# Attention with its branch and output products taken per two query tiles, as seven half products for eight

## The reference

```python
a = dsa_attention(q, k, v, qi, ki, wi, k_sel) * jax.nn.silu(z_a)
b = multiscale_pool(u_b, pool_w[layer], pool_scale[layer]) * jax.nn.silu(z_b)
g = jax.nn.sigmoid(gates.reshape(B, S, N_BRANCHES, D_MODEL) + merge_bias[layer])
y = g[:, :, 0] * (a @ w_branch_a[layer]) + g[:, :, 1] * (b @ w_branch_b[layer])
x = x + y @ w_out[layer]
```

## Time and profile before

| | |
|---|---|
| median of 3 runs | 3606.58 us (3606.16 to 3606.78) |
| span of the profiled execution, first to last instruction | 3598.9 us |
| what the runs have around that span | 7.7 us |
| TensorE busy | 3489.8 us, 97% of the span |
| VectorE, ScalarE, GpSimd busy | 1897.1, 1626.0, 416.8 us |
| start of `attention` to the end | 2709.4 to 3598.9, that is 889.5 us |

### The profile page before, as it was taken

How to read it: one execution, slowest core, us unless ns; L and a number is a source line. 1 busy time by engine, 2 the same in 40 slices (tenths; PEclk the granted TensorE clock), 3 DMA queues, 4 the chain that set the end, 5 groups by cost and what they waited for, 6 DMA issues and landing times. The chain is left out here.

```text
span 3598.9 us, 70546 instructions
## 1 busy us (share of the span) xinstructions
PE 3489.8 (97%) x28700; PEld 2709.4 (75%) x28700; DVE 1897.1 (53%) x4784; ACT 1626.0 (45%) x3703; POOL 416.8 (12%) x690
## 2 busy tenths in 40 slices
PE   6999999996999999999999999999999999999998
PEld 5888988885666666578778887777886677777765
DVE  5223332346777777534788788666683333333322
ACT  2222333324445444313677666777763334443320
POOL 0000000004554544310000000000000000000000
PEclk9999999998999999999999999999999999999999
DMA  9111111114222222241111114121215212111121
GB/s 310 60 48 54 54 54 54 54 76 139 72 92 91 82 77 77 91 132 48 50 54 62 53 52 168 57 66 61 69 47 194 79 48 78 42 50 67 50 82 41
DMA packets 142357, 282.08 MB, mean 78 GB/s; under 512 B 35056, under 2 KB 94464, under 8 KB 134528
## 3 DMA queue, kind: packets, MB, share of 16 engines
q1 hardware_dynamic: 133360, 267.75, 21.3%
q0 software_dynamic: 2304, 8.39, 0.6%
q10 hardware_dynamic: 6416, 2.08, 0.2%
HBM read 181.72 MB, written 96.47 MB: 77 GB/s over the span
## 5 line engine op out<-in xcount | busy, mean ns | idle before, releaser
L2598 ACT ACTIVATE at_pT<-at_bank 128x512 f32<-128x512 f32 (+3 forms) x320 | 154.4, 531 | 532.1 <-PE at_bank L2497 531.8
L1992 PEld LDWEIGHTS p_bank<-p_hT,w_in_rest 128*128 128x128 f32 x3072 | 345.4, 192 | 14.0 <-issue 12.4
L1992 PE MATMUL p_bank<-p_hT,w_in_rest 128*128 128x128 f32 x3072 | 349.9, 276 | 1.3 <-DVE p_st L2276 1.3
L325 PE MATMUL p_bank<-p_hT,w_in_rest 128*128 128x128 f32 x2720 | 349.1, 275 | 0.0
L325 PEld LDWEIGHTS p_bank<-p_hT,w_in_rest 128*128 128x128 f32 x2720 | 326.4, 192 | 0.0
L2113 ACT ACTIVATE p_r<-p_acc,p_mid 128x384 f32<-128x384 f32 (+13 forms) x224 | 292.9, 1308 | 58.7 <-DVE p_acc L2303 54.4
L1983 PE MATMUL p_bank<-arena,p_hT 128*128 128x512 f32 (+2 forms) x768 | 242.8, 468 | 1.3 <-ACT p_hT L2107 1.3
L2538 PE MATMUL at_bank<-arena,at_y 128*128 128x512 f32 x512 | 239.8, 599 | 4.1 <-DVE at_y L2648 2.5
L2173 ACT ACTIVATE p_r<-p_bank,ahead_rows 128x512 f32<-128x512 f32 (+3 forms) x304 | 168.1, 635 | 156.2 <-PE p_bank L2086 144.3
L325 PE MATMUL p_bank<-p_hT,arena 128*128 128x128 f32 x1632 | 229.0, 276 | 4.0 <-ACT p_hT L421 3.0
L2074 PE MATMUL p_bank<-p_hTg,arena 128*128 128x256 f32 x1024 | 226.7, 381 | 1.7 <-ACT arena L2135 1.7
(11 more groups left out here) (428 smaller groups left out, 6264.5 us busy)
## 6 DMA issues: line engine op xcount, KB each, us to landing
stage<-p_st SPq DMA_DIRECT2D x15, 1856.0 KB, 5.9
arena<-stage SPq DMA_DIRECT2D x15, 1856.0 KB, 7.6
at_rest<-stage SPq DMA_DIRECT2D x16, 1280.0 KB, 5.9
stage<-x_or_pr SPq DMA_DIRECT2D x128, 128.0 KB, 1.8
p_ada<-in_ada_w SPq DMA_DIRECT2D x8, 1024.0 KB, 9.6
p_xt<-in_x SPq DMA_DIRECT2D x16, 512.0 KB, 3.2
x_or_pr<-in_x SPq DMA_DIRECT2D x16, 512.0 KB, 3.2
x<-x_or_pr SPq DMA_DIRECT2D x16, 512.0 KB, 3.3
```

Of the source, the lines that this page charges most:

```text
L325: last = mm(out, w_in(k, at, at + P), hT[:, k, 1:P + 1], start=(k == 0), stop=(k == KD - 1))
L1992: last = mm(bank[:, m * P:(m + 1) * P], weights(k, c + m * P, c + (m + 1) * P), hTs[:, n % 2, k, :], start=(k == 0), stop=(k == KD - 1))
L2598: f(flat(pT[:, g, at // P:(at + wide) // P, :]), TURNED[j % 2][:, 0:wide], ACT.Copy).then_inc(S["pT_taken"], 1)
```

## The change

The dense products are no longer made per tile but per pair of tiles that follow each other in `ORDER` (e = 0, 1). For a product of a pair, the activation (256 tokens by the contraction) and the weight are each cut into 2 x 2 blocks, and Strassen's scheme in Winograd's form replaces the eight block products by seven. The seven half products of a kind are named by a digit: b1 to b7, a1 to a7, p1 to p7. A branch half product has 8 matmuls of 128 columns, an output one 4 matmuls of 512 columns. So a pair has 14 branch and 7 output products, where it had 8 branch halves of 16 matmuls and 4 output halves of 8.

- **Weights.** The sums of weight blocks are made once, in the gate phase: SP loads 16 pieces (4 of b, 4 of a, 8 of the output weight; four blocks of 256 columns each), POOL makes four sums of 128 x 256 for each, and SP stores them to a DRAM tensor `combined`. One piece is begun at every seventh chunk n, and stored four chunks later. The attention reads `combined` in 14 slots of 1 MB per pair (two branch products share a slot, an output product has one) through a ring of 5 slots, so 14 MB per pair and 112 slots in all.
- **Activations.** POOL makes four sums of 128 x 256 for b and for a (`T`), and four of 128 x 512 for y (`Sy`).
- **Results.** DVE takes each product out of PSUM and adds it into its block (`take`, 24 instructions per pair where there were 16); the gates, the sum of both branches and the sum with x go from DVE to POOL: `gated_b`, `gated_a`, `out_sum`.
- **Order.** The dense products of pair m run in the eight steps of the tiles of pair m+1, two or three in a step, by the tables `DENSE_EARLY` and `DENSE_LATE`; eight steps after the last tile serve the last pair alone. From the last pair of tiles on (`DENSE_LATE`), the uses rotate over three banks, two of them taken from the four score banks; until then all share one as before. The first product of a step stands ahead of the values product, except where d does.

```diff
+                def fetch_piece(e):
+                    kind, part = PIECES[e]
+                    if e == 0:
+                        sp.wait_ge(S["zb_done"], TILES)
+                    from_one(sp, S["piece_stored"], 16 * e)
+                    load = lambda dst, src: sp.dma_start(dst, src).then_inc(S["piece_loaded"], 16)
+                    k, at = part // 2, part % 2 * PIECE_W
+                    for i, (row_half, column_half) in PIECE_PLACES[kind]:
...
+                            load(pieces[:, i, :], A["w_out_2"][0][(4 * row_half + k) * P:(4 * row_half + k + 1) * P, c:c + PIECE_W])
+                        elif kind == "b":
+                            load(pieces[:, i, :], A["w_branch_b_2"][0][(2 * row_half + k) * P:(2 * row_half + k + 1) * P, c:c + PIECE_W])
+                        else:
+                            for g in range(A2_KV):
+                                r = 256 * g + HEAD * (2 * row_half + k)
+                                load(pieces[HEAD * g:HEAD * g + HEAD, i, :], A["w_branch_a_2"][0][r:r + HEAD, c:c + PIECE_W])
...
+                def store_piece(e):
...
+                    sp.wait_ge(S["piece_combined"], e + 1)
+                    sp.dma_start(combined[:, at:at + 7 * w].rearrange("p (i w) -> p i w", w=w)[:, :, part * PIECE_W:(part + 1) * PIECE_W], pieces[:, 0:7, :]).then_inc(S["piece_stored"], 16)
...
+                        if n >= 2 and n - 2 < 7 * len(PIECES):
+                            if (n - 2) % 7 == 0:
+                                fetch_piece((n - 2) // 7)
+                            if (n - 2) % 7 == 4:
+                                store_piece((n - 2) // 7)
...
+                def combine(e):
...
+                    if PIECES[e][0] == "o":
+                        tt(part(3), part(6), part(7), ALU.subtract)
+                        ch.link(tt(part(5), part(7), part(0), ALU.subtract))
+                        ch.link(tt(part(2), part(6), part(5), ALU.subtract))
+                        tt(part(4), part(2), part(1), ALU.subtract).then_inc(S["piece_combined"], 1)
...
+HALVES = (1, 2, 6, 7, 4, 5, 3)
...
+LATE_PAIR = PAIRS - 1
+DENSE_EARLY = (("b1", "b2", "b6"), ("b7", "b4", "b5"), ("b3", "a1", "a2"), ("a6", "a7", "a4"), ("a5", "a3", "p1"), ("p2", "p6"), ("p7", "p4"), ("p5", "p3"))
+DENSE_LATE = (("b1", "b6", "b7"), ("b2", "b5", "b4"), ("b3", "a1", "a6"), ("a7", "a2", "a5"), ("a4", "a3", "p1"), ("p2", "p6"), ("p7", "p5"), ("p4", "p3"))
+LATE_BANK = {"d": 0, "1": 0, "2": 0, "6": 1, "7": 2, "5": 1, "4": 2, "3": 1}
...
+                def fetch_x(m):
+                    from_one(sp, S["out_stored"], 32 * m)
+                    for e in range(2):
+                        load("x_loaded", o[:, e, :], x1[rows_of(ORDER[2 * m + e]), :])
+
+                def fetch_weights(k):
+                    if k >= RING_W:
+                        sp.wait_ge(S["spare_done"], USES.last_of_slot[k - RING_W])
+                    at = k % SLOTS_W * SLOT_W
+                    load(f"w_loaded{k % RING_W}", ring[:, k % RING_W, :], combined[:, at:at + SLOT_W])
...
+                for step in range(STEPS + BLOCKS_OF):
...
+                        fetch_za(n)
+                    if step % BLOCKS_OF == 2 and 2 <= step // BLOCKS_OF <= PAIRS:
+                        fetch_x(step // BLOCKS_OF - 1)
+                    if step % BLOCKS_OF == 5 and 1 <= step // BLOCKS_OF < PAIRS:
+                        fetch_rest(step // BLOCKS_OF)
+                    while fetched < SLOTS_W * PAIRS and step >= BLOCKS_OF and USES.last_of_slot[fetched - RING_W] <= max(place[name, step // BLOCKS_OF - 1] for name in dense_of(step)) + 1:
+                        fetch_weights(fetched)
+                        fetched += 1
...
+                def moving_sums(half):
+                    tt(T[:, 2, :], half(1, 1), half(1, 0), ALU.subtract)
+                    ch.link(tt(T[:, 0, :], half(1, 0), half(0, 0), ALU.subtract))
+                    ch.link(tt(T[:, 1, :], half(1, 1), T[:, 0, :], ALU.subtract))
+                    tt(T[:, 3, :], T[:, 1, :], half(0, 1), ALU.subtract).then_inc(S["T_ready"], 1)
+
+                def stationary_sums(m):
+                    pool.wait_ge(S["y_added"], 4 * m + 4)
+                    from_one(pool, S["spare_done"], place["p3", m - 1] + 1 if m > 0 else 0)
+                    y11, y12, y21, y22 = (y[:, e, k, :] for e in range(2) for k in range(2))
+                    ch.link(tt(Sy[:, 0, :], y21, y22, ALU.add))
+                    ch.link(tt(Sy[:, 1, :], Sy[:, 0, :], y11, ALU.subtract))
+                    tt(Sy[:, 2, :], y11, y21, ALU.subtract)
+                    tt(Sy[:, 3, :], y12, Sy[:, 1, :], ALU.subtract).then_inc(S["Sy_ready"], 1)
+
...
+                def gated_b(name, m):
+                    e, half = WHERE[name[1]]
+                    pool.wait_ge(S["spare_taken"], place[name, m] + 1)
+                    tt(yb[:, e, half, :], yb[:, e, half, :], gate("b", e, half), ALU.mult).then_inc(S["yb_ready"], 1)
+
+                def gated_a(name, m):
+                    e, half = WHERE[name[1]]
+                    pool.wait_ge(S["spare_taken"], place[name, m] + 1)
+                    pool.wait_ge(S["yb_ready"], 4 * m + 4)
+                    ch.link(tt(y[:, e, half, :], y[:, e, half, :], gate("a", e, half), ALU.mult))
+                    tt(y[:, e, half, :], y[:, e, half, :], yb[:, e, half, :], ALU.add).then_inc(S["y_added"], 1)
+
+                def out_sum(name, m):
+                    e, half = {"p2": (0, 0), "p4": (1, 0), "p5": (1, 1), "p3": (0, 1)}[name]
+                    part = yb[:, half, e, :]
+                    c = slice(512 * half, 512 * half + 512)
+                    pool.wait_ge(S["spare_taken"], place[name, m] + 1)
+                    pool.wait_ge(S["x_loaded"], 32 * (m + 1))
+                    tt(o[:, e, c], o[:, e, c], part, ALU.add).then_inc(S["o_added"], 1)
...
+                def spare_for(name, of):
+                    from_one(pe, S["spare_taken"], USES.free[name, of])
+                    bank = USES.bank[name, of]
+                    if bank:
+                        pe.wait_ge(S["masked"], 2 * LATE_BLOCK)
+                    return SPARE[bank]
...
+                        pe.wait_ge(S["T_ready"], 2 * m + (1 if name[0] == "b" else 2))
+                        src = T[:, {5: 0, 6: 1, 7: 2, 4: 3}[q], :]
+                    src = src.rearrange("p (k t) -> p k t", t=P)
+                    for b in range(4):
+                        for k in range(2):
+                            last = mm(bank[:, b * P:(b + 1) * P], w[:, k, b * P:(b + 1) * P], src[:, k, :], start=(k == 0), stop=(k == 1))
+                        if b == 3:
+                            last.then_inc(S["spare_done"], 1)
+                        yield
...
+                    else:
+                        pe.wait_ge(S["Sy_ready"], m + 1)
+                        src = Sy[:, {5: 0, 6: 1, 7: 2, 3: 3}[q], :]
+                    src = src.rearrange("p (k t) -> p k t", t=P)
+                    for k in range(4):
+                        last = mm(bank[:, :], src[:, k, :], w[:, k, :], start=(k == 0), stop=(k == 3))
+                        if k == 3:
+                            last.then_inc(S["spare_done"], 1)
...
+                    first, others = dense(step, names[:1]), dense(step, names[1:])
+                    left = 4 * len(names[1:])
...
                         turn_denominators(n - 1)
-                    if 0 <= step - 1 < STEPS:
-                        values(step - 1)
+                        if step - 1 < STEPS:
+                            values(step - 1)
+                        for _piece in first:
+                            pass
+                    else:
+                        for _piece in first:
+                            pass
...
-                def gate_b(n, half):
-                    k = 7 * n + 1 + half
-                    dve.wait_ge(S["spare_done"], k + 1)
-                    dve.wait_ge(S["rest_loaded"], 16 * (n + 1))
-                    tt(flat(yb[:, 4 * half:4 * half + 4, :]), SPARE[:, :], gates[:, 1024 + half * 512:1536 + half * 512], ALU.mult).then_inc(S["spare_taken"], 1)
...
-                def gate_a(n, half):
-                    k = 7 * n + 3 + half
-                    mine = flat(y[:, 4 * half:4 * half + 4, :])
-                    dve.wait_ge(S["spare_done"], k + 1)
-                    tt(mine, SPARE[:, :], gates[:, half * 512:half * 512 + 512], ALU.mult).then_inc(S["spare_taken"], 1)
-                    dve.wait_ge(S["spare_taken"], k + 1)
-                    tt(mine, mine, flat(yb[:, 4 * half:4 * half + 4, :]), ALU.add).then_inc(S["y_ready"], 1)
...
+                def take(name, m):
...
+                    dve.wait_ge(S["spare_done"], place[name, m] + 1)
+                    dve.wait_ge(S["spare_taken"], place[name, m])
+                    if q == 1:
+                        if kind == "b":
+                            from_one(dve, S["o_added"], 4 * m)
+                        if kind == "p":
```

(17 more changed lines are left out.)

298 lines of the change are left out of this document (187 added, 111 removed).

## The result

The changed kernel takes 3584.24 us (median of 4 runs, 3578.9 to 3590.39), the kernel before 3606.37 beside it (3602.02 to 3606.78): 0.9939 of its time, 95% interval 0.9925 to 0.9953. It is faster by 22 us, where 49 were forecast, and lies 8 us above the range.

The account below looks back on a forecast made before the run. TensorE, busy 97% of the span, was taken to bound the kernel. The terms -57.0 + 1 + 0.5 + 1 + 1 + 4.8 = -48.7 us gave 3558 us, range 3549 to 3576.

Parts of the forecast that it names:

- -57 us ... I count it whole: Attention's dense work: seven products for eight save 7.1 us a pair over eight pairs, all on full PE.
- +0.5 for hand-overs in the middle: Tiles 6 to 7: attention work between products covers PSUM bank hand-overs; 0.5 us lost, bounds 0 and 34.
- would cost nothing, since after the change DVE's long instructions there have at most one input in SBUF: Attention: DVE and POOL locking each other out of SBUF was priced at nothing.
- +1 for tile 4 alone: Tile 4, now without dense work: PE and ACT close together, 1 us more idle, bounds 0 and 4.
- +1 for tiles 5 and 3: Tiles 5 and 3: two products stand back to back in tile 3's one block; 1 us for both tiles.
- +1 for tiles 1 and 0: Tiles 1 and 0: POOL's chains add waits, three banks remove hand-overs; net 0.4, rounded up to 1 us.
- +4.8 behind the last tile: Behind the last tile: hand-overs saved 4.9 us; stalls of 3.5 and 4.7 and a 1.5 us later end added.
- 0 for DMA: Attention: 14 MB of weights per pair stay hidden by a small margin, at no cost.
- 0 for the gate phase: Gate phase: POOL's 64 weight sums and SP's extra loads and stores cost 0, upper bound 10 us.
- the weight ring binds: Rival, chance 0.05: products wait for weight slots at slow landing rates, making the kernel slower than before.
- The middle loses hand-overs: Rival, chance 0.20: middle tiles lose hand-overs and POOL's chains bind more often; 3566 to 3582 us.
- The record counts: Profile sign: branch matmul records go from 2048 to 1792, the output's from 512 to 448.

Follow-up runs that it names:

- e6: e2 with each step's first dense product put straight ahead of the transposes again, as in the kernel before; 3585.49 us, ratio 0.9943 to the kernel before.
- e7: Changed kernel with late products in early order, separate sum signals, part of POOL's late work on DVE, and e2's copy; 3563.69 us, ratio 0.9887.
- e2: Changed kernel with DVE's copy of the reciprocals made by a tensor_scalar that also writes an accumulator; 3580.71 us, ratio 0.9934 to the kernel before.
- e4: Kernel before with one unused POOL multiplication per tile, released by DVE's last take of the tile; 3615.63 us, ratio 1.0027.
- e10: e7 with the first five weight slots and first x loaded after tile 4's queries; 3558.89 us, ratio 0.9867 to the kernel before.
- e3: Changed kernel with 14 and 13 unused matmuls filling PE's stalls ahead of a6 and p2 behind the last tile; 3583.22 us, ratio 0.9941.
- e8: Changed kernel loading only an eighth of each weight slot in the attention, so its output is wrong; 3580.33 us, ratio 0.9928 to the kernel before.
- e1: Kernel before's attention with the changed kernel's gate phase, its weight sums stored but not read; 3604.22 us, ratio 0.9996 to the kernel before.

## Why the prediction was wrong

Two steps failed.

**The first step that failed is "-57 us ... I count it whole", with the +0.5 for hand-overs in the middle.** It priced undisturbed records and left out what a product pays at its places in a step. Over four pairs the dense products fell from 231.1 to 207.6 us (table), 23.5 less where 28.4 were counted, since 56 products of 1.91 us and 28 of 3.59 stand where 1.825 and 3.43 were assumed, while the old halves were nearer to their price (3.70 for 3.65, 7.04 for 6.87). The places are the reason: 116 at 0.10 us where there were 68 (e6). The transposes with the waits behind them are 3.4 us longer in e7 than in before. Of this 2.8 are longer waits for DVE's takes, which the prediction put at nothing in the middle, "a group of six to eight transposes" being enough; six last 0.66 us and eight 0.87, and the next product starts 1.00 us behind the start of the group. The rest comes from groups that now stand behind scores or values, where eight take 0.93 us. So e7, without the copy's lock, is 19.6 us under before in the eight tiles instead of 28.4. Why PE pays the 0.10 us (tile shape, bank or weight load) no experiment isolates. The pairs of narrow tiles lose more than the 2.2 us a pair of these: 102.4 us for 99.3 in tiles 6 and 8, 86.8 for 82.3 in 5 and 3 (e7). Added up in the same way, their dense products fell by 5.7 and 5.2 instead of 7.1, their transposes grew by 1.1 and 1.9, and the scores, values and d by 0.5 and 0.8.

**The second step that failed is the sentence that the lock "would cost nothing, since after the change DVE's long instructions there have at most one input in SBUF".** The copy at L2666, now L2913, has one SBUF input and is short, and it is locked all the same: 0.43 us becomes 1.49 in most tiles. The forecast moved the takes' partners to POOL without asking what stands on DVE right behind a take. It costs 8.2 us of the attention part (e2), 7.3 of them in the twelve tiles from 6 to 3, where nothing else differs, and e4 shows it in the kernel before. The Trainium skill has both halves of it: "SBUF — State Buffer", section "Who interferes with whom", says that a `copy` can run in a mode that takes the ports shared with GpSimd, that the first to issue keeps them for its whole instruction, and that `tensor_scalar` with an accumulator written out does not take them. The trace agrees in each: 1483 ns behind POOL's sum, 686 with the accumulator form. I had used that page for two-input instructions only.

**+1 for tile 4 alone:** 21.4 us from d group to d group, where 46.4 - 28.35 + 1 = 19.1 were forecast. The thin overlap of ACT and PE that I had named is there, four waits of 0.73 us on `at_pT` (2.9 us where before had none), and 1.6 us is the wait on `at_qT`, a DMA; e10 removes that one.

**+1 for tiles 5 and 3:** they lost 5.2. Of these 0.6 are gone in e7, with d's wait; the rest is the pattern above.

**+1 for tiles 1 and 0:** 3.6. The stall on `T` was there (2.2 us, 2 forecast), and d waited too. Behind the stall the clock fell (0.95 in both windows), which the sum did not have.

**+4.8 behind the last tile:** 7.7. The stalls were sized well, a6's 3.40 us (3.5 forecast) and p2's 3.21 (4.7 for p2 and p6). Not in the sum was that PE runs at 1.2 GHz behind each: 2.8 and 3.0 us, 4.5 of which e3 got back. The stall of 3.4 us cost 6.2.

**0 for DMA:** right in the middle and at the end (e8; no wait on `arena`); wrong by 1.6 us at the start, where the ring's first loads stand ahead of the queries. In its sum for tiles 1 and 0, 76.4 less 7 is 69, not 66, so the 290 GB/s become 274; 224 and 297 were measured. **0 for the gate phase:** right (e1). The rival "the weight ring binds" is out. "The middle loses hand-overs" came nearest in its time (3582), and in part by its mechanism: the late starts. The record counts came as said: 1024, 384 and 384 of the branch matmuls are 1792, 256 and 192 of the output's 448.

**The 32.0 us missed in the attention part**, taken apart: 7.3 are the copy's lock in twelve tiles (after against e2). 8.4 are the places and late starts in the eight tiles of the table, beyond 0.4 of the 0.5 forecast; 6.5 are the same pattern in tiles 6, 8, 5 and 3. 2.5 and 2.9 are tiles 1 and 0 and the end, where the lower clock behind the stalls is more than the whole difference; 2.3 are tile 4, and 2.1 tile 2's clock, which was low by chance in this execution.

## What to carry to other kernels

When work is moved to GpSimd, look at what VectorE does in the next microsecond after the instruction that releases it, short copies included; the form with an accumulator costs 0.26 us more by itself and was 0.8 us faster here. Price a saved matmul at its place: here each switch between the dense work and scores or values cost 0.10 us, and so did each start behind a wait, so seven products for eight gave about 10% and not 12.5%. Short waits that a list of waits leaves out are found by adding up from start to start. And price a TensorE stall of about three microseconds at one and a half times to near double (3.4 us cost 5.1 in e8, 6.2 in after), because the matmuls behind it ran at the lower clock; another product in that place was worth more here than less work on the producer.

## What the hardware showed that I had not expected

- A VectorE copy of 128 x 512 that starts 0.06 us behind a GpSimd sum of 1.27 us takes 1.49 us instead of 0.43; the same values by `tensor_scalar` with an accumulator take 0.686 us in every case.
- Sixteen GpSimd instructions of 1.03 us, on data of their own, slowed an otherwise unchanged kernel by 0.27%.
- A dense product of 16 records on TensorE takes 1.79 us between transposes, 1.89 with scores (64 rows) on one side, 1.99 between values and scores; eight records behind a wait of 0.24 us take 1.00 instead of 0.89.
- TensorE behind stalls of 3.40 and 3.21 us: granted clock 0.54 and 0.50 over the next 4 us, 32 records in 6.33 us instead of 3.57; after e8's stalls of the same length 5.27 us.
- Traffic into SBUF of 144 or 61 GB/s beside full TensorE: 66.00 us in both.
